# First attention's scores in two fp32r passes over stacked high and low parts; the gate block on TensorE's column groups

## The reference, cut to what matters

```python
mod = jax.nn.silu(c) @ w_ada[l] + b_ada[l]
sh1, sc1, gt1, sh2, sc2, gt2 = [m[:, None, :] for m in jnp.split(mod, 6, axis=-1)]
...
q = apply_rope(q.reshape(bsz, seq, N_HEADS, HEAD_DIM), cos, sin)
k = apply_rope(k.reshape(bsz, seq, N_KV_HEADS, HEAD_DIM), cos, sin)
...
s_loc = jnp.einsum('bnqkgd,bnjkd->bnkgqj', qb, kb).astype(jnp.float32) * scale
s_ctx = jnp.einsum('bnqkgd,bjkd->bnkgqj', qb, k_ctx).astype(jnp.float32) * scale
...
p = jax.nn.softmax(jnp.concatenate([sk, s_ctx, s_loc], axis=-1), axis=-1)
...
x = x + gt2 * expert_choice_ffn(h2, w_router[l], w_gate[l], w_up[l], w_down[l])
```

## Time and profile before

| | us |
|---|---|
| median of 3 runs (lowest, highest) | 2507.57 (2504.72, 2509.72) |
| the profiled execution | 2506.87 |
| its span | 2505.1 |
| stretch of the input projections (first strip to last) | 41 to 157 |
| stretch of the first attention | 159 to 239 |
| stretch of the output projection | 239 to 285 |
| routing, then experts, to about | 755 |
| TensorE busy over the span | 2470.1 (99%) |
| VectorE, ScalarE, GpSimd busy | 1131.5, 736.6, 49.5 |

### The profile page before, as it was taken

How to read it: one execution, slowest core, us unless ns; L and a number is a source line. 1 busy time by engine, 2 the same in 40 slices (tenths; PEclk the granted TensorE clock), 3 DMA queues, 4 the chain that set the end, 5 groups by cost and what they waited for, 6 DMA issues and landing times.

```text
span 2505.1 us, 29717 instructions
## 1 busy us (share of the span) xinstructions
PE 2470.1 (99%) x11265; PEld 1805.7 (72%) x11265; DVE 1131.5 (45%) x1730; ACT 736.6 (29%) x1051; POOL 49.5 (2%) x28
## 2 busy tenths in 40 slices
PE   8999999999999999999999999999999999999999
PEld 4876744444437888888888888888887667888887
DVE  6786412222227544436444334444337665544422
ACT  4245210100014332224333223233224354333321
POOL 0032000000000000000000000000000000000000
PEclk9999999999999999999999999999999999999999
DMA  7552699999992223323223322223322211223332
GB/s 309 177 177 80 261 409 420 421 421 421 422 408 96 100 100 102 103 63 102 100 92 106 105 83 92 97 95 105 103 86 71 80 43 41 95 92 100 105 104 68
DMA packets 84654, 404.29 MB, mean 161 GB/s; under 512 B 9176, under 2 KB 9560, under 8 KB 60896
## 3 DMA queue, kind: packets, MB, share of 16 engines
q1 hardware_dynamic: 84576, 403.22, 43.2%
HBM read 401.08 MB, written 2.10 MB: 161 GB/s over the span
## 4 chain that ended last, share of the span: by engine, by line
PE 92%; DVE 3%; ACT 2%; issue 1%; ACTq 0%; DVEq 0%
PE pair L1144 23%; PE pair L1146 23%; PE pair L1145 23%; PE pair L1436 9%; PE pair L1461 4%; PE pair L1372 2%; PE pair L1400 1%; PE pair L1691 1%; PE pair L1829 1%; PE pair L1487 1%; PE pair L1286 1%; PE pair L1799 1%; PE pair L1800 1%; PE pair L1401 1%; DVE prob L2078 0%
## 5 line engine op out<-in xcount | busy, mean ns | idle before, releaser
L1854 DVE TENSOR_TENSOR wL<-stage,wH 128x1024 fp32r<-128x1024 f32 (+3 forms) x301 | 388.9, 1292 | 774.4 <-ACT wH L699 774.0
L1144 PE MATMUL pair<-hH,wH 128*128 128x512 f32 x1672 | 657.9, 393 | 7.5 <-DVE hL L1963 2.2
L1146 PE MATMUL pair<-hH,wL 128*128 128x512 f32 x1672 | 651.4, 390 | 0.0
L1145 PE MATMUL pair<-hL,wH 128*128 128x512 f32 x1672 | 651.4, 390 | 0.0
L699 ACT ACTIVATE wH<-stage 128x1024 fp32r<-128x1024 f32 (+3 forms) x301 | 335.3, 1114 | 845.1 <-PE pair L1146 841.6
L1144 PEld LDWEIGHTS pair<-hH,wH 128*128 128x128 f32 x1672 | 314.3, 188 | 78.4 <-DVE hL L1899 3.8
L1145 PEld LDWEIGHTS pair<-hL,wH 128*128 128x128 f32 x1672 | 314.3, 188 | 66.7 <-issue 2.4
L1146 PEld LDWEIGHTS pair<-hH,wL 128*128 128x128 f32 x1672 | 314.3, 188 | 66.0
L1144 PE MATMUL pair<-gH,wH 128*128 128x512 f32 x704 | 273.9, 389 | 0.0
L1145 PE MATMUL pair<-gL,wH 128*128 128x512 f32 x704 | 273.9, 389 | 0.0
L1146 PE MATMUL pair<-gH,wL 128*128 128x512 f32 x704 | 273.9, 389 | 0.0
(11 more groups left out here) (365 smaller groups left out, 2150.9 us busy)
## 6 DMA issues: line engine op xcount, KB each, us to landing
ring<-in_experts SPq DMA_DIRECT2D x182, 1024.0 KB, 19.7
stage<-in_gate SPq DMA_DIRECT2D x88, 512.0 KB, 3.2
stage<-in_up SPq DMA_DIRECT2D x88, 512.0 KB, 3.2
stage<-in_down SPq DMA_DIRECT2D x64, 704.0 KB, 4.0
adaw<-in_w_ada SPq DMA_DIRECT2D x32, 512.0 KB, 4.9
stage<-in_w_in SPq DMA_DIRECT2D x18, 512.0 KB, 3.7
ring<-in_experts SPq DMA_DIRECT2D x16, 512.0 KB, 11.4
stage<-in_mla_in SPq DMA_DIRECT2D x9, 512.0 KB, 3.2
```

What stands on the lines that cost most here:

```text
L1144: pe.matmul(ps, lh, rh, start=first, stop=False)
L1145: pe.matmul(ps, lh, rl, start=False, stop=False)
L1146: return pe.matmul(ps, ll, rh, start=False, stop=last)
L1854: dve.tensor_tensor(low, stage[:, n % STAGE, 0:w], high, ALU.subtract).then_inc(strip_lo, 1)
```

## The change

It does three things. **Scores:** each query tile is split into a high and a low part (ACT `high_part`, DVE `low_half`, one buffer `part_q`, for the keys `part_k`), and SP moves the parts within SBUF (`stacked`): for a head, the high part of its queries onto one half of the partitions and the low part onto the other (`qS`), and the keys' high part onto both halves and their low part onto both (`kS`). A score product is then two fp32r matmuls over all 128 partitions. Keys of the context and latent keys lie in one row, so that a block's scores are one or two pieces (`key_pieces`), and one load brings all masks. **Gate block:** POOL's work goes; SP loads the eight gate tiles during steps 2 to 9, and PE makes four matmuls of each behind strips 3 to 10, one on each group of 32 columns (`gate_part`); ACT copies the sum, PE turns it (`gate_turn`), DVE adds the bias, and the first scores wait for that. **Places:** the strips of the first 26 numbers use smaller staging and part tiles within the same memory, to make room; some semaphores are joined.

The diff, cut to its core (the renamed semaphores, and waits on them, are left out):

```diff
-        gate_w = [place(f"gate_w{j}", [P, 1024], F32, at) for j, at in enumerate((G + 20 * KB, G + 35 * KB))]
-        gate_acc = place("gate_acc", [P, 1024], F32, TM + 7 * TILE)
+        gate_w = [place(f"gate_w{j}", [P, 1024], F32, at) for j, at in enumerate((G, G + 4 * KB))]
+        gate_row = place("gate_row", [P, 256], F32, G + 85 * KB)
         qT = place("qT", [P, 4, T], F32, G + 56 * KB)
-        kT = place("kT", [P, T], F32, G + 64 * KB)
-        kZ = place("kZ", [P, 2, T + C], F32, G + 48 * KB)
-        window_first = place("window_first", [P, C + 2 * P], F32, G + 54 * KB)
+        kT = place("kT", [P, C + T], F32, G + 64 * KB)
+        part_q = place("part_q", [P, 2, T], F32R, TM + 5 * TILE)
+        part_k = place("part_k", [P, 2, C + T], F32R, G + 8 * KB)
+        qS = [place("qS0", [P, 4, T], F32R, TM), place("qS1", [P, 4, T], F32R, G + 48 * KB)]
+        kS = place("kS", [P, 2, 2, C + T], F32R, G + 120 * KB)
         vT = place("vT", [P, T + C], F32, G + 67 * KB)
...
                 return firstH[:, n - FFN1A, :], firstL[:, n - FFN1A, :]
+            if n < FFN1A:
+                return w4H[:, n % 2, :], w4L[:, n % 2, :]
             return wH[:, n % 2, 0:width[n]], wL[:, n % 2, 0:width[n]]
...
+        GATE_AT = 2
+        MASK_AT = (5 * P, 0, C, 0)
+        MOVES = 16 * (4 * 4 + 8)
...
-        kv_tiles = {n: [4, 5] + list(range(keys(n)[0] // P, keys(n)[1] // P)) for n in range(NB)}
+        kv_tiles = {0: [4, 5, 0, 1], 1: [4, 5, 0, 1, 2], 2: [1, 2, 3, 4, 5], 3: [4, 5, 2, 3]}
+
+        def key_pieces(n):
+
+            return {0: [(0, 0, 512)], 1: [(128, 0, 384), (512, 384, 256)], 2: [(128, 384, 384), (512, 0, 256)],
+                    3: [(0, 0, 256), (256, 512, 256)]}[n]
+
+        def masked_scores(u):
+
+            n, a, j = UNITS[u]
+            w = C + keys(n)[1] - keys(n)[0]
+            first = key_pieces(n)[0][0]
+            return pair[j][:, first:first + w], window[:, MASK_AT[n]:MASK_AT[n] + w]
...
+            def stacked(r):
+
+                sp.wait_ge(qk_lo, r + 1)
+                for part in range(2):
+                    if r == K_AT:
+                        for j in range(2):
+                            for at in range(0, P, 64):
+                                sp.dma_start(kS[at:at + 64, j, part, :].bitcast(F32), part_k[64 * j:64 * j + 64, part, :].bitcast(F32)).then_inc(qk_moved, 16)
+                    else:
+                        for j in range(2):
+                            at = 64 * (j ^ part)
+                            sp.dma_start(qS[j][at:at + 64, ROT_Q[r], :].bitcast(F32), part_q[64 * j:64 * j + 64, part, :].bitcast(F32)).then_inc(qk_moved, 16)
+
             def gate_tile(j):
 
-                if j == 0:
-                    sp.wait_ge(strip_used, V_AT + 1)
+                if j < 2:
+                    sp.wait_ge(h_lo, LO0[NCTX] + KD)
                 else:
-                    sp.wait_ge(ada_added, max(24, 2 * j + 21))
+                    sp.wait_ge(gate_used, j - 1)
                 sp.dma_start(gate_w[j % 2][:, :], A["w_ada"][j * P:j * P + P, 5 * 1024:6 * 1024]).then_inc(gate_landed[j % 2], 16)
...
+                if GATE_AT <= s < GATE_AT + KD:
+                    gate_tile(s - GATE_AT)
+                if s - 2 in ROT_AT:
+                    stacked(ROT_AT[s - 2])
+                if s == 12:
+                    sp.wait_ge(v_turned, 2)
+                    sp.dma_start(window[:, :], A["window"]).then_inc(window_loaded, 16)
...
-            for j in range(KD):
-                pool.wait_ge(gate_landed[j % 2], 16 * (j // 2 + 1))
-                if j == 0:
-                    pool.tensor_scalar(gate_acc[:, :], gate_w[0][:, :], stat[:, 0:1], None, ALU.mult).then_inc(ada_added, 1)
-                else:
-                    w = gate_w[j % 2]
-                    pool.tensor_scalar(w[:, :], w[:, :], stat[:, j:j + 1], None, ALU.mult).then_inc(ada_added, 1)
-                    pool.wait_ge(ada_added, 24 + 2 * j)
-                    pool.tensor_tensor(gate_acc[:, :], gate_acc[:, :], w[:, :], ALU.add).then_inc(ada_added, 1)
-            pool.wait_ge(ada_added, GATES)
+            pool.wait_ge(strip_used, 18)
+            pool.wait_ge(mod_ready, 5)
             pool.memset(keep[:, :, :], 1.0).then_inc(cleared, 1)
-            pool.wait_ge(cleared, 3)
+            pool.wait_ge(cleared, 1)
             pool.memset(keep[:, :, 0:1], 0.0).then_inc(cleared, 1)
...
+            def high_part(r):
+
+                act.wait_ge(rope_done, r + 1)
+                if r == K_AT:
+                    act.wait_ge(strip_used, V_AT + 1)
+                    ins = act.activation(part_k[:, 0, :], kT[:, :], ACT.Copy)
+                else:
+                    if r:
+                        act.wait_ge(qk_moved, 64 * r if r < K_AT else 64 * (r + 1))
+                    ins = act.activation(part_q[:, 0, :], qT[:, ROT_Q[r], :], ACT.Copy)
+                ins.then_inc(qk_hi, 1)
+
             for s in range(18):
                 hi(s + 2)
                 copy_out(s)
+                if s - 1 in ROT_AT:
+                    high_part(ROT_AT[s - 1])
+                if s == 12:
+                    act.wait_ge(gate_used, KD)
+                    act.activation(gate_row[:, :], pb[6][:, 0:256], ACT.Copy).then_inc(gate_rowed, 1)
...
+            def gate_part(j):
+
+                pe.wait_ge(gate_landed[j % 2], 16 * (j // 2 + 1))
+                if j == 0:
+                    pe.wait_ge(std_done, NCTX + 1)
+                for g in range(4):
+                    mm = pe.matmul(pb[6][32 * g:32 * g + 32, 0:256], stat[:, j:j + 1].broadcast_to([P, 32]), gate_w[j % 2][:, 256 * g:256 * g + 256],
+                                   start=(j == 0), stop=(j == KD - 1))
+                mm.then_inc(gate_used, 1)
+
+            def gate_turn():
+
+                pe.wait_ge(gate_rowed, 1)
+                for i in range(2):
+                    mm = pe.transpose(pb[6][:, 256 + i * P:256 + (i + 1) * P], gate_row[:, i * P:(i + 1) * P], tab("ident"))
+                mm.then_inc(mod_summed, 1)
...
+                if GATE_AT < s <= GATE_AT + KD:
+                    gate_part(s - GATE_AT - 1)
                 if s in SUM_AT:
                     mod_sum(SUM_AT[s])
+                if s == 17:
+                    gate_turn()
                 if s == 9:
...
                 if u < 2:
                     pe.wait_ge(out_taken, 18)
-                    pe.wait_ge(rope_done, 5)
-                    pe.wait_ge(cleared, 2)
+                    pe.wait_ge(qk_moved, MOVES)
+                    pe.wait_ge(mod_ready, 6)
...
-                q = qT[:, a, n * P:(n + 1) * P]
-                pe.matmul(pb[2 * j][:, 0:C], q, kZ[:, j, T:T + C], start=True, stop=True)
-                mm = pe.matmul(pb[2 * j][:, C:2 * C], q, kZ[:, j, lo_:lo_ + C], start=True, stop=True)
-                if hi_ - lo_ > C:
-                    mm = pe.matmul(pb[2 * j + 1][:, 0:hi_ - lo_ - C], q, kZ[:, j, lo_ + C:hi_], start=True, stop=True)
+                q = qS[j][:, a, n * P:(n + 1) * P]
+                for at, key, w in key_pieces(n):
+                    pe.matmul(pair[j][:, at:at + w], q, kS[:, j, 0, key:key + w], start=True, stop=False)
+                    mm = pe.matmul(pair[j][:, at:at + w], q, kS[:, j, 1, key:key + w], start=False, stop=True)
                 mm.then_inc(scored, 1)
...
-            pe.wait_ge(ada_added, GATES)
-            pe.wait_ge(shift_copied, 1)
-            for m in range(KD):
-                mm = pe.matmul(pb[3][:, m:m + 1], gate_acc[:, m * P:(m + 1) * P], ones[:, 0:1], start=True, stop=True)
-            mm.then_inc(mod_summed, 1)
...
-                if r0 == K_AT:
-                    dve.tensor_tensor(kZ[0:64, 0, 0:T], dst[0:64, :], tmp[0:64, :], ALU.add)
-                    dve.tensor_tensor(kZ[64:128, 1, 0:T], dst[64:128, :], tmp[64:128, :], ALU.add).then_inc(rope_done, 1)
+                dve.tensor_tensor(dst, dst, tmp, ALU.add).then_inc(rope_done, 1)
+
+            def low_half(r):
+
+                dve.wait_ge(qk_hi, r + 1)
+                if r == K_AT:
+                    ins = dve.tensor_tensor(part_k[:, 1, :], kT[:, :], part_k[:, 0, :], ALU.subtract)
                 else:
-                    dve.tensor_tensor(dst, dst, tmp, ALU.add).then_inc(rope_done, 1)
+                    ins = dve.tensor_tensor(part_q[:, 1, :], qT[:, ROT_Q[r], :], part_q[:, 0, :], ALU.subtract)
+                ins.then_inc(qk_lo, 1)
 
             for s in range(2, 18):
...
+                if s - 2 in ROT_AT:
+                    low_half(ROT_AT[s - 2])
...
+            def by_group(v):
+
+                return v.rearrange("p (g i) -> p i g", i=2)
+
+            dve.wait_ge(mod_summed, 6)
+            bias = cols[:, COL["b_ada"][0] + 40:COL["b_ada"][0] + 48]
+            dve.tensor_tensor(by_group(mod[:, 40:48]), pb[6][:, 256:512].rearrange("p (i g r) -> p i g r", i=2, g=4)[:, :, :, 0], by_group(bias), ALU.add)\
+               .then_inc(mod_ready, 1)
...
```

(3 more changed lines are left out.)

100 lines of the change are left out of this document (44 added, 56 removed).

## The result

| | before | after |
|---|---|---|
| median, us (lowest to highest, 4 runs each) | 2506.85 (2504.72 to 2509.72) | 2557.32 (2554.92 to 2558.22) |
| span of the profiled execution | 2505.1 | 2556.2 |
| start of the last column sums of the projections | 157.44 | 213.05 |
| first softmax | 161.85 | 218.94 |
| first output projection behind the last values | 239.47 | 291.15 |

What follows compares the result with a forecast made beforehand. TensorE, without a gap in the projections and near full in the first attention, was taken as the bound; tile waits 25.75 + gate matmuls 4.8 - attention 6.6 = +23.95 us on 2506.87, say 2531, range 2514 to 2545.

Runs made afterwards that it cites:

- the gate block alone: Kernel before with only the change's gate block, scores, keys and queries as before: 2540.57 us; with needless matmuls ahead of four tile waits 2533.81 us.

## What to carry to other kernels

A transfer between halves of the partitions takes more of the transfer engines than its bytes say (here 1.6 times), and in the stretches where such moves ran beside loads all of them together got little more than half the rate; write in place what needn't cross, and move only the rest. A load that a full engine waits for belongs behind nothing that waits for a third engine, and its landing time is that of the queue ahead of it, not the median of its kind. Where a step is put on an engine without gaps, look first for a place where that engine waits anyway: the same gate matmuls cost some 0.4 us at the two ends of the attention (last value product to output projection: 5.4 us where it was 5.1).

## What the hardware showed unexpectedly

- Moves within SBUF from one half of the partitions to the other: 207 to 211 GB/s at share 0.91, 128 partitions 385 at 1.07, and 1.6 times the engine time for the same bytes; one issue took SyncE 0.6 us for either, mostly 0.33 to 0.43 for a load of 512 KB.
- Four 32-column fp32 products of 256 columns took 0.57 us with the step to the next strip, 0.48 in a row (1.93 for four tiles): they run beside each other.
- After each wait of 3.9 to 11.5 us TensorE ran for 3.4 to 6.3 us at the 1.2 GHz level; with waits covered by needless matmuls the gate block alone lost 0.7 us to it instead of 6.5.
